# Weight sums of the gate/up pairs by an ACT copy and an accumulating POOL DMA, with a new order of steps, and later mixes in the output stage

## The reference

```python
def first_block(x, p, ...):
    h = x
    y = _rms(h, norm_mix_g)
    z = y @ w_in                       # four mixers: oa, ob, oc, od
    h = h + concatenate([oa, ob, oc, od]) @ w_out
    y = _rms(h, norm_ffn_g)
    h = h + (silu(y @ w_gate) * (y @ w_up)) @ w_down
    y = _rms(h, norm_ple_g)
    h = h + sigmoid(y @ w_ple_gate) * (p @ w_ple_proj)
    return _rms(h, final_norm_g)

def swa_sink_mixer(h, w_in, ..., w_out):   # the second block
    ...
    return (o * jax.nn.silu(gate)) @ w_out
```

## Time and profile before

| | |
|---|---|
| median of 3 runs | 1395.29 us |
| the profiled execution | 1396.01 us, of which the span of the page is 1394.3 us |
| PE busy | 1385.0 us, 99% of the span |
| DVE busy | 1146.4 us, 82% |
| ACT busy | 788.3 us, 57% |
| POOL busy | 79.5 us, 6% |
| granted PE clock | 1.0 throughout |
| DMA | 318.32 MB, mean 228 GB/s |

### The profile page before, as it was taken

The page is one execution under the profiler, slowest core; times in us unless marked ns, Lnnn a source line. Parts: engine busy times, 40 slices in busy tenths (PEclk is TensorE's granted clock), DMA queues, the critical chain, the costliest instruction groups (busy, mean ns, idle before and its releaser), DMA issues.

```text
span 1394.3 us, 16628 instructions
## 1 busy us (share of the span) xinstructions
PE 1385.0 (99%) x6239; PEld 1133.1 (81%) x6239; DVE 1146.4 (82%) x1355; ACT 788.3 (57%) x1074; POOL 79.5 (6%) x64
## 2 busy tenths in 40 slices
PE   9999999999999999999999999999999999999998
PEld 7888888888888888888888888888878887777886
DVE  6589976767999988999998889977677669887796
ACT  7476755554565544565555455555465556675453
POOL 2000010000000000000000000000000144420000
PEclk9999999999999999999999999999999999999999
DMA  9766656774775746675685655686877678889654
GB/s 334 246 208 212 206 169 204 257 245 133 263 247 191 234 170 224 232 243 194 212 269 185 226 211 196 212 296 208 284 249 278 220 260 258 268 260 298 193 187 151
DMA packets 171753, 318.32 MB, mean 228 GB/s; under 512 B 11953, under 2 KB 35757, under 8 KB 171544
## 3 DMA queue, kind: packets, MB, share of 16 engines
q1 hardware_dynamic: 156792, 285.37, 61.9%
q10 hardware_dynamic: 13088, 25.18, 5.8%
q0 software_dynamic: 1792, 6.71, 1.5%
HBM read 293.04 MB, written 24.17 MB: 228 GB/s over the span
## 4 chain that ended last, share of the span: by engine, by line
PE 90%; DVE 6%; DMA 2%; ACT 1%; issue 1%; SPq 0%; POOL 0%; ACTq 0%; DVEq 0%; POOLq 0%
PE acc L1924 15%; PE acc L1926 14%; PE acc L1925 14%; PE acc L2110 12%; PE acc L2113 12%; PE acc L2112 12%; DVE w_lo L1198 3%; PE acc L1986 1%; PE tp L2110 1%; PE tp L2113 1%; PE tp L2112 1%; PE sp L2113 1%; PE sp L2112 1%; PE sp L2110 1%; DMA parked<-tile 1%; PE sp L2214 1%
## 5 line engine op out<-in xcount | busy, mean ns | idle before, releaser
L795 ACT ACTIVATE w_hi<-w_raw 128x1024 fp32r<-128x1024 f32 x541 | 564.8, 1058 | 462.1 <-PE acc L1926 229.2
L1198 DVE TENSOR_TENSOR w_lo<-w_raw,w_hi 128x1024 fp32r<-128x1024 f32 x530 | 639.8, 1226 | 175.6 <-ACT w_hi L795 171.2
L1924 PE MATMUL acc<-w_lo,hh 128*128 128x512 f32 x528 | 207.9, 394 | 0.0
L1926 PE MATMUL acc<-w_hi,hl 128*128 128x512 f32 x528 | 205.7, 390 | 0.0
L1925 PE MATMUL acc<-w_hi,hh 128*128 128x512 f32 x528 | 205.6, 389 | 0.0
L2110 PE MATMUL acc<-w_lo,yh 128*128 128x512 f32 x460 | 179.7, 391 | 0.6 <-DVE w_lo L1198 0.6
L2112 PE MATMUL acc<-w_hi,yh 128*128 128x512 f32 x460 | 179.0, 389 | 0.0
L2113 PE MATMUL acc<-w_hi,yl 128*128 128x512 f32 x460 | 179.0, 389 | 0.0
L1924 PE MATMUL acc<-w_lo,yh 128*128 128x512 f32 x416 | 162.4, 390 | 1.1 <-DVE w_lo L1198 1.1
L1926 PE MATMUL acc<-w_hi,yl 128*128 128x512 f32 x416 | 161.9, 389 | 0.0
L1925 PE MATMUL acc<-w_hi,yh 128*128 128x512 f32 x416 | 161.9, 389 | 0.0
(11 more groups left out here) (277 smaller groups left out, 1756.1 us busy)
## 6 DMA issues: line engine op xcount, KB each, us to landing
w_raw<-in_w_gate SPq DMA_DIRECT2D x88, 512.0 KB, 5.5
w_raw<-in_w_up SPq DMA_DIRECT2D x88, 512.0 KB, 6.5
w_raw<-in_w_down SPq DMA_DIRECT2D x88, 512.0 KB, 5.9
w_raw<-in_w_in SPq DMA_DIRECT2D x64, 512.0 KB, 4.6
w_raw<-in_swa_w_in ACTq DMA_DIRECT2D x48, 512.0 KB, 5.2
w_raw<-in_w_out SPq DMA_DIRECT2D x32, 512.0 KB, 5.0
w_raw<-in_w_ple_gate SPq DMA_DIRECT2D x32, 512.0 KB, 6.1
w_raw<-in_swa_w_out SPq DMA_DIRECT2D x32, 512.0 KB, 5.8
```

The source lines that it names most:

```text
L795: act.activation(w_hi[:, v % SPL], w_raw[:, s % RAW], ACT.Copy).then_inc(hi_ready, 1)
L1198: dve.tensor_tensor(w_lo[:, v % SPL], w_raw[:, s % RAW], w_hi[:, v % SPL].bitcast(F32), ALU.subtract).then_inc(lo_ready, 1)
L1924: pe.matmul(dst, xh[:, f, tk], w_lo[:, v % SPL, k], start=(f == 0), stop=False)
L1926: last = pe.matmul(dst, xl[:, f, tk], w_hi[:, v % SPL, k], start=False, stop=(f == CK * n - 1))
```

## The change

**Pairs.** The sums of a set move to the tile `wide`, in two buffers of 2048 elements used in turn. ACT copies the two raw tops of the set (1024 elements, `copy_tops`, L870 in the changed kernel) into the middle of the buffer; POOL issues a DMA that adds u's raw chunk (128 rows of 4 KB) to it; DVE does two additions of 512 elements, `sum_weights` (L1289) after the step given by `summed`, and `last_sum` (L1302) after the low part of the next step. DVE's instruction of 1024 elements is gone. Steps t and s are split from `wide`. The raw slots of g and u are free after the sums, not after the low parts of t and s. Signs change from subtractions to additions where the sums did.

```diff
-PAIR_PLAN = plain(0, 3) + quad("g", 0) + plain(0, 4) + quad("u", 0) + plain(0, 5) + quad("t", 0) + quad("s", 0)
...
+PAIR_PLAN = plain(0, 4, 3) + quad("g", 0) + plain(1, 4) + quad("g", 1) + quad("g", 2) + quad("u", 0) + quad("t", 0)
...
+SUMS = dict(copied={1: [0], 6: [1], 11: [2]}, summed={0: 5, 1: 11, 2: 15})
...
-SO_AT = [dict(scale=2, turn=4, gated=12, low=13, m1=13, mix=16, mixed_gate=17, mixed_up=18, bank=19, put=10, fetch=10),
-         dict(add=1, m1=11, mix=14, mixed_gate=15, mixed_up=16, bank=17)]
+SO_AT = [dict(scale=2, turn=4, gated=12, high=14, low=14, m1=13, mix=17, mixed_gate=18, mixed_up=19, bank=19, put=10, fetch=10),
+         dict(add=1, m1=11, mix=16, mixed_gate=17, mixed_up=18, bank=19)]
...
+            for i, (a, b) in enumerate(BY_DMA):
+                pool.wait_ge(tops_copied, i + 1)
+                pool.dma_start(wide[:, i % 2, CW:3 * CW], w_raw[:, b % RAW].rearrange("p k n -> p (k n)"),
+                               accum_op=ALU.add).then_inc(tops_added[i % 2], 16)
...
+            def copy_tops(b, q):
...
+                for s in (g, u):
+                    act.wait_ge(raw_in[s % RAW], 16 * (s // RAW + 1))
+                if i == 0:
+                    act.wait_ge(proj_out, 16 * NG)
+                if i >= 2:
+                    wait_low(act, SPLITS.index(("s",) + BY_DMA[i - 2]))
+                act.activation(weight_sums(g, u)[:, 1:3], w_raw[:, g % RAW:g % RAW + 2, 0],
+                               ACT.Copy).then_inc(tops_copied, 1)
...
+                if v - 1 in SUMMED_AT:
+                    last_sum(*SUMMED_AT[v - 1])
+                if v in SUMMED_AT:
                     wait_low(dve, v)
-                    sum_weights(a, b)
+                    sum_weights(*SUMMED_AT[v])
...
+                if (a, b) in BY_DMA:
+                    i, into = BY_DMA.index((a, b)), weight_sums(a, b)
+                    dve.wait_ge(tops_added[i % 2], 16 * (i // 2 + 1))
+                    dve.tensor_tensor(into[:, 3], u[:, 1], into[:, 1], ALU.add).then_inc(w_sums, 1)
+                    return
```

More of the change, by code:

```diff
@@ L120 @@
               + plain(1, 7, 4, 2) + plain(0, 6) + plain(1, 6, 3)]
[L122 to L125, removed]
+SUMS = dict(copied={1: [0], 6: [1], 11: [2]}, summed={0: 5, 1: 11, 2: 15})
+PAIR_AT = {0: dict(add=1, m1=12, mix=19, gate=20, silu=21, **SUMS),
+           1: dict(hidden=1, turn=2, m1=12, mix=19, gate=20, low=21, silu=21, put=9, fetch=12, **SUMS),
+           2: dict(hidden=1, sums=4, turn=5, m1=12, mix=19, gate=20, low=21, silu=21, put=10, fetch=13, **SUMS),
+           3: dict(hidden=1, turn=2, m1=12, sums_high=17, mix=19, gate=20, sums_low=21, low=21, silu=21, put=9, fetch=12,
+                   **SUMS)}
 DOWN_AT = [dict(hidden=1, turn=3, low=13, m1=14, mix=15, mixed_gate=16, bank=18, mixed_up=19, put=9, fetch=11),
@@ L173 @@
         OWN[_b] = LAST_READ[_b] = _v
-    if _kind == "t":
+QUADS = sorted((_a, _b) for _kind, _a, _b in SPLITS if _kind == "u")
+W_SUMS = {}
+SUMMED_AT = {}
+BY_DMA = []
+_sums = 0
+for _block in BLOCKS:
+    if "summed" in _block.at:
+        BY_DMA += [(_block.raw + _block.loads.index(("g", _q)), _block.raw + _block.loads.index(("u", _q))) for _q in _block.quads]
+for _v, (_kind, _a, _b) in enumerate(SPLITS):
+    if _kind == "u" and (_a, _b) not in BY_DMA:
+        SUMMED_AT[_v] = (_a, _b)
+for _block in BLOCKS:
+    for _q, _i in _block.at.get("summed", {}).items():
+        SUMMED_AT[_block.v0 + _i] = (_block.raw + _block.loads.index(("g", _q)), _block.raw + _block.loads.index(("u", _q)))
+for _v in sorted(SUMMED_AT):
+    W_SUMS[SUMMED_AT[_v]] = _sums + (2 if SUMMED_AT[_v] in BY_DMA else 3)
+    _sums = W_SUMS[SUMMED_AT[_v]]
+for _v, (_kind, _a, _b) in enumerate(SPLITS):
+    if _kind == "t" and (_a, _b) not in BY_DMA:
         LAST_READ[_b] = _v
-    if _kind == "s":
+    if _kind == "s" and (_a, _b) not in BY_DMA:
         LAST_READ[_a] = _v
-QUADS = [(_a, _b) for _kind, _a, _b in SPLITS if _kind == "u"]
+LAST_SUM = {}
+for _a, _b in BY_DMA:
+    LAST_SUM[_a], LAST_SUM[_b] = W_SUMS[_a, _b], W_SUMS[_a, _b] - 1
 QUAD_BLOCKS = [b for b in BLOCKS if b.quads]
@@ L409, in build @@
         w_sums = sem("w_sums")
+        proj_out = sem("proj_out")
+        proj_in = sem("proj_in")
+        tops_copied = sem("tops_copied")
+        tops_added = [sem(f"tops_added{i}") for i in range(2)]
         m1_copied = sem("m1_copied")
@@ L1165, in _ @@
                         og_high(2)
-                    if i == b.at.get("low"):
+                    if i == b.at.get("high"):
                         og_high(3)
@@ L2149, in block @@
                     if kind == "s":
-                        product(m5, sums(q, 3), v, 0)
-                        last = product(gate_[1], tokens(q, 1, 1), v, 1)
+                        k = int(SPLITS[v][1:] in BY_DMA)
+                        product(m5, sums(q, 3), v, k)
+                        last = product(gate_[1], tokens(q, 1, 1), v, 1 - k)
                     if by_bank is None or i < len(b.plan) - 1:
```

88 lines of the change are left out of this document (59 added, 29 removed).

## The result

The changed kernel takes 1403.7 us (median of 4 runs, 1403.54 to 1404.91); the kernel before took 1395.2 us beside it (4 runs). The ratio is 1.0057, with a 95% interval of 1.0042 to 1.0072: slower, by about 8 us. The prediction was 1403.1 us. In the later run `after_again` the ratio was 1.0053 (1.0038 to 1.0068).

A forecast was written before the change was run, and what follows sets the result against it. PE bounds the kernel, busy 1385.0 of 1394.3 us, so only its late starts count. Terms 9.0 + 1.1 + 1.0 - 1.3 - 2.05 = +7.8 us give 1403.1 by the median; range 1399 to 1410.

The forecast's parts named there:

- The chain at s2: Third set of each pair: handovers from t2's split to s2's low part make PE 0.90 us late, 9.0 in ten.
- Hidden sums in pairs 3 and 7: ACT's copy of the hidden sums right behind s2's split makes step 18 0.57 us late; 1.1 in two pairs.
- Pairs 2 and 6: Four more DVE instructions and later loads bring ACT to t2 later: 0.5 us a pair, 1.0 in all.
- old late starts: Six late PE starts in the pairs of the kernel before, 1.8 us, all taken as gone; 1.3 gained net.
- The accumulating DMA: POOL's 512 KB addition in each set lands in 7 to 8 us, within the 9.1 allowed, and costs nothing.
- past 9.1 each further us costs one us in each pair: If the accumulating DMA takes over 9.1 us, t2's split waits for it, one us per further us.
- rival B: The accumulating DMA takes over 9.1 us: 1412 at 10 us, 1426 at 11.4; chance 0.17 (over 1410).
- Wide parked and fetched: Four writes and four reads of the tile wide, the reads in the last down product: cost 0, high end 3.
- Output stage: Late starts in two blocks: 0.85 falls to about 0.25 and 1.45 goes; gain 2.05 us, ends 1.4 and 2.3.
- Totals: Thirty sets: DVE loses about 37 us of sums, ACT gains 32 us of copies; neither on the path outside the chain.
- A: The chain at s2 is not there, so the change only gains: 1391.4 us at best, 1392.5 with remainders; chance 0.12.
- C: Half of the chain: s2 late by 0.3 us a pair, 1397 us; chance 0.07 (1393 to 1399).

The follow-up runs named there:

- after_again: The changed kernel, unchanged, run again with another profile; 1404.2 us, ratio 1.0053 to the kernel before.
- sum_ahead: The changed kernel with the third set's last sum made ahead of t2's low part in each pair; 1392.9 us, ratio 0.9973 to the kernel before.
- longer_chain: The changed kernel with the third set's last sum made twice in each pair, the second waiting for the first; 1413.2 us, ratio 1.0118 to the kernel before.
- pairs_alone: The changed kernel with the output stage's positions of before; 1405.9 us, ratio 1.0065 to the kernel before.
- old_plan_new_sums: The pairs' step order and positions of before, with the new sums, last sum ahead where t follows, and the changed output stage; 1432.2 us, ratio 1.0261.
- output_alone: The kernel before with only the new positions of the output stage; 1395.5 us, ratio 0.9987 to the kernel before.
- late_copy: sum_ahead with ACT's copy for the third set two steps later, ahead of step 13's split; 1406.3 us, ratio 1.0070 to the kernel before.
- new_plan_old_sums: The changed kernel with an empty table of sums: new step order, all three sums of a set by DVE in the raw buffers; 1454.6 us, ratio 1.0415.
- copy_12: sum_ahead with ACT's copy for the third set one step later, ahead of step 12's split; 1391.9 us, ratio 0.9967 to the kernel before.

## Why the prediction was right, point by point

The prediction has +7.8 us; the change measured +8.0 by the ratio and +7.5 in the span. Its main term is right in its mechanism, handover by handover. That the sum is as near as it is owes something to luck: smaller terms were off both ways, and two places that nobody had named cancelled.

- **The chain at s2**: predicted 0.79 + 0.11 = 0.90 a pair, measured 0.82 + 0.11 = 0.93 in eight pairs. Handover by handover, from T: split 0.49 (measured 0.48), low part 1.58 (1.57), last sum 2.71 (2.72), split of s2 3.42 (3.44), low part 4.51 (4.53), PE 5.78 (5.81), due 4.99 (4.99). sum_ahead and longer_chain show it to be the cause, from both sides.
- **Hidden sums in pairs 3 and 7**: predicted 0.57, measured 0.51. That it is part of the same chain was not said; it went with sum_ahead.
- **Pairs 2 and 6**: predicted 0.5 more each, measured 0.31 more at s2 and 0.32 at another place, t0 of the first set. The reasons named are those seen (loads that land late ahead of t2, four more instructions on DVE), and the size was near; but t0, where DVE's instructions count, was not named. The old late starts all went, 1.87 (the one at 582 us cost 0.19 and not 0.11), where 1.3 net was predicted. Pairs in all: +9.8 predicted, +9.7 measured, since too little was added for the chain and for these two pairs (0.3 each) and too little taken off for the old late starts (0.6).
- **The accumulating DMA**: predicted 7 to 8 us, cost 0; measured 6.6 in the median and 8.5 at most, cost 0. For the third set the 9.1 us till DVE wants the result were 1 too many: the split and the low part of u2 are 512 elements, 0.6 and 0.7 us long, and the sum took 1.06 and 1.22 for them. In pair 1 POOL issued at 351.51 and DVE came to the sum at 359.60, 8.1 us on; no landing of a third set took over 7.6 in the changed kernel, so this did no harm. In pair 1 of pairs_alone one took 8.7: DVE waited 0.73 us for it, and s2 came 0.09 later than in the changed kernel. So for this set a landing begins to cost some 0.5 us sooner than predicted. The step behind it, "past 9.1 each further us costs one us in each pair", was tried only with the last sum ahead: there nearly all of the cost came in the two pairs where ACT comes late to the copy and SP's fetches fall beside the DMA. The Trainium skill ("DMA: Bandwidth & Descriptors", section on the anatomy of a SWDGE DMA) gave an estimate of 3.2 to 4.4 us; by that the minimum of 4.5 is near, and the median, beside other transfers, is 2.2 us above. Its page "SBUF — State Buffer" (section "SBUF: two separate sides") gave rival B its mechanism, about 10 us behind low parts of DVE. It says this of VectorE operations in a 2-port performance mode, and the prediction did not show that low parts are of that kind. The longest of thirty was 8.5, and 9.8 in old_plan_new_sums; no run here shows what such a landing waited for.
- **Wide parked and fetched**: predicted 0; no late start is seen in the last down product.
- **Output stage**: predicted -2.05, measured -2.05 in the trace, and -1.8 by the times of output_alone. The 0.25 that is left stands one step behind the place for which it was predicted.
- **Totals**: DVE 35 us less (37 predicted), ACT 26 more (32 predicted). As said there, neither counts for the time.
- **Not spoken of**: -1.1 and +0.75 at two places that the change does not touch. They cancelled nearly; had they not, the sum would have been off by about 1 us.
- **Rivals**: A (no chain) and C (half of it) fell by the ten rows at `tp`, B by the landings. Rival A's number, 1391.4 to 1392.5, is what the same change gives when the chain is taken away by another order: 0.9973 of 1395.3 is 1391.5.

## What to carry to other kernels

Before you take an instruction off a busy engine, ask in what order the rest of it stands: here 35 us of DVE's work went, and one 0.68 us sum on the wrong side of a low part cost 11 us. Where a step's operand is computed between two short steps, sum the handovers from the slot's release to PE, and compare with the matmuls in between; if the sum is longer, look for idle time of the same engine ahead of its last input, and move the instruction there. A place in the order that fits most repeats of a loop may be too late in the few where an engine comes to it late (pairs 2 and 6 of late_copy). A table of numbers that sets the order is tested cheapest at the one place where products get short.

## What the runs showed of the hardware

- A late start of PE costs 0.10 to 0.12 us more than its own length: the second start behind it comes 0.33 to 0.34 us on, where the pace is 0.2267. This held in every late start in the pairs at full clock.
- PE's granted clock fell to 0.50 with single idle times of 3.9 and 4.2 us (late_copy), 3.3, 4.6 and 3.1 (old_plan_new_sums) and 1.92 (new_plan_old_sums, 397.52 us), each behind a stretch at 1.0. It stayed at 1.0 with idle times of 2.0 us (longer_chain), 2.5 (old_plan_new_sums, 624.53 us) and again 1.92 (new_plan_old_sums, 672.67 us). So among waits of 1.9 to 2.5 us the length alone does not tell whether the clock falls. In late_copy the half clock added 1.5 us to the wait of 3.9 and 2.4 to that of 4.2.
- An accumulating DMA of 512 KB within SBUF, issued by POOL in 0.86 us, landed in 4.5 to 8.5 us in the changed kernel, beside loads of the same size with medians of 5.4 to 5.9; the longest in the other kernels of the new order was 8.7 (copy_12), and 9.8 in any run (old_plan_new_sums).
